# One hybrid attention layer: short attention groups drawn over four ticks, the drain of their sums moved behind the transposed scores, and the split output weights moved from SyncE's queue to ScalarE's

## The reference

```
h = rmsnorm(x); proj = h @ w_in            # q, k, v of 8 stick-breaking heads, q, k, v and gates of 8
                                           # forgetting heads, q of 4 memory heads, a gate over all 20
stick-breaking: A[t,s] = sigmoid(z) * prod_{s<j<t} sigmoid(-z),  s < t, out = A @ v
forgetting:     softmax(q.k + cumulated log forget gates), s <= t,  out = P @ v
memory:         softmax(q.k) over 256 memory rows,                  out = P @ v
y = per-head rmsnorm(outputs) * silu(gate)
out = rmsnorm(x + y @ w_out)
```

## Time and profile before

| | |
|---|---|
| median of 3 runs | 841.03 us |
| the profiled execution | 841.03 us, its span 839.3 us |
| PE busy | 806.2 us (96%) |
| DVE, ACT, POOL busy | 583.5, 474.8, 257.7 us |
| chain that ended last | PE 75%, DVE 11%, ACT 6% |
| mean granted TensorE clock | 0.993 |

### The profile page before, as it was taken

The page is one execution under the profiler, slowest core; times in us unless marked ns, Lnnn a source line. Parts: engine busy times, 40 slices in busy tenths (PEclk is TensorE's granted clock), DMA queues, the critical chain, the costliest instruction groups (busy, mean ns, idle before and its releaser), DMA issues.

```text
span 839.3 us, 12264 instructions
## 1 busy us (share of the span) xinstructions
PE 806.2 (96%) x4244; PEld 676.9 (81%) x4244; DVE 583.5 (70%) x1207; ACT 474.8 (57%) x938; POOL 257.7 (31%) x382
## 2 busy tenths in 40 slices
PE   8899999999999999999999999999999989989996
PEld 7677787887878888887888888788888877878884
DVE  5746667557577877767787776878666584874575
ACT  5756776755855555685555568554555763532231
POOL 1135514232156223415622342562223111420000
PEclk9999999999999999999999999999999998999998
DMA  8125652203313121411312141132213397142532
GB/s 302 52 76 168 203 207 76 72 18 89 114 50 77 53 111 64 120 45 51 76 62 101 64 125 39 52 81 65 93 52 76 125 354 249 34 167 76 176 126 100
DMA packets 35533, 88.95 MB, mean 106 GB/s; under 512 B 3592, under 2 KB 11784, under 8 KB 34448
## 3 DMA queue, kind: packets, MB, share of 16 engines
q1 hardware_dynamic: 35472, 88.17, 31.6%
HBM read 57.72 MB, written 21.53 MB: 94 GB/s over the span
## 4 chain that ended last, share of the span: by engine, by line
PE 75%; DVE 11%; ACT 6%; issue 3%; POOL 3%; DMA 1%; SPq 0%; DVEq 0%; ACTq 0%; POOLq 0%
PE banks L745 13%; PE banks L747 12%; PE banks L746 12%; PE banks L786 9%; PE banks L886 7%; PE banks L906 4%; PE banks L905 4%; PE banks L873 4%; PE banks L872 4%; DVE work L1543 2%; PE banks L926 2%; POOL w_parts L1304 1%; DVE pT L1580 1%; DVE work L1546 1%; DMA work<-in_x 1%
## 5 line engine op out<-in xcount | busy, mean ns | idle before, releaser
L745 PE MATMUL banks<-hT,w_parts 128*128 128x512 f32 x576 | 240.0, 417 | 9.3 <-POOL w_parts L1304 3.2
L747 PE MATMUL banks<-hT,w_parts 128*128 128x512 f32 x576 | 226.1, 392 | 0.0
L746 PE MATMUL banks<-hT,w_parts 128*128 128x512 f32 x576 | 225.3, 391 | 0.0
L1580 DVE TENSOR_TENSOR pT<-banks,pT 128x512 fp32r<-128x512 f32 x208 | 109.1, 563 | 84.2 <-ACT pT L1103 83.1
L1103 ACT ACTIVATE pT<-banks 128x512 fp32r<-128x512 f32 x208 | 93.4, 498 | 130.2 <-PE banks L886 129.6
L745 PEld LDWEIGHTS banks<-hT,w_parts 128*128 128x128 f32 x576 | 108.6, 188 | 26.2 <-DVE fx_heads L1480 4.0
L747 PEld LDWEIGHTS banks<-hT,w_parts 128*128 128x128 f32 x576 | 108.1, 188 | 24.4
L1304 POOL TENSOR_TENSOR w_parts<-w_raw,w_parts 128x1024 fp32r<-128x1024 f32 x37 | 88.8, 2400 | 114.7 <-ACT w_parts L1006 114.7
L746 PEld LDWEIGHTS banks<-hT,w_parts 128*128 128x128 f32 x576 | 109.0, 189 | 12.7
L1079 ACT ACTIVATE work<-banks 128x512 f32<-128x512 f32 (+2 forms) x96 | 47.5, 495 | 96.6 <-PE banks L873 87.6
L1543 DVE TENSOR_TENSOR_SCAN work<-work 128x639 f32<-128x639 f32 (+3 forms) x64 | 92.6, 1446 | 7.2 <-POOL work L1312 7.1
(11 more groups left out here) (213 smaller groups left out, 1395.6 us busy)
## 6 DMA issues: line engine op xcount, KB each, us to landing
w_raw<-in_w_tiles SPq DMA_DIRECT2D x37, 512.0 KB, 3.6
hT<-wo_dram SPq DMA_DIRECT2D x16, 512.0 KB, 7.6
fx_heads<-fx_heads SPq DMA_DIRECT2D x8, 512.0 KB, 7.3
negL<-negL_dram SPq DMA_DIRECT2D x8, 512.0 KB, 7.1
yT_dram<-silu SPq DMA_DIRECT2D x8, 512.0 KB, 5.2
sb_heads<-sb_heads SPq DMA_DIRECT2D x8, 512.0 KB, 7.1
negL<-yT_dram SPq DMA_DIRECT2D x8, 512.0 KB, 5.0
work<-in_x SPq DMA_DIRECT2D x6, 512.0 KB, 6.4
```

Of the source, the lines that this page charges most:

```text
L745: pe.matmul(o, w[:, 0, k, :], hT[:, 0, k, tok], start=(k == 0), stop=False)
L746: pe.matmul(o, w[:, 0, k, :], hT[:, 1, k, tok], start=False, stop=False)
L747: mm = pe.matmul(o, w[:, 1, k, :], hT[:, 0, k, tok], start=False, stop=(k == KT - 1))
L1580: dve.tensor_tensor(pT[:, n % 3, 1, cols], banks[:, T_BANK + n % 2, cols], pT[:, n % 3, 0, cols].bitcast(F32), ALU.subtract).then_inc(t_lo, 1)
```

## The change

Three edits.

1. `t_tick`: the steps of a c=0 group of fx and sb lie one in each of the ticks 4g+5 to 4g+8. The planner, which reads `t_tick`, moves some parts with it.
2. The ten loads and twenty stores of output weight halves, with their waits, go from SP to ACT, in the ticks in which they stood, behind the sigmoids or exponentials (a store behind the rounding, too).
3. `output_lo` on ACT and `output` on DVE stand behind the transposed scores and the small piece of their tick.

```diff
@@ t_tick
-    return 4 * t.group + 5 + (t.s // 2 if x.c else t.s // 2 * 2)
+    return 4 * t.group + 5 + (t.s // 2 if x.c else t.s)
@@ sync: functions load_w_out_half, store_w_out_half and their calls removed
-                for n, half in enumerate(W_OUT_HALF):
-                    if i == half.load:
-                        load_w_out_half(n)
-                    if i == half.store:
-                        store_w_out_half(n)
@@ scalar: the same functions, with act. for sp.
+            def load_w_out_half(i):
+                x, n = W_OUT_HALF[i], halves_before(i)
+                if n:
+                    act.wait_ge(wo_half_out[x.place], 32 * n)
...
+                act.dma_start(wo_half_rows[x.place][0], w_out[...]).then_inc(wo_half_in[x.place], 16)
+            def store_w_out_half(i):
+                x = W_OUT_HALF[i]
+                raw, hi = wo_half_rows[x.place]
+                act.wait_ge(wo_lo, len(W_OUT_AT) + i + 1)
+                act.dma_start(wo_dram[x.j, 0, :, ...], hi).then_inc(wo_half_out[x.place], 16)
+                act.dma_start(wo_dram[x.j, 1, :, ...], raw).then_inc(wo_half_out[x.place], 16)
@@ scalar, tick loop
                 for n, x in enumerate(W_OUT_HALF):
+                    if i == x.load:
+                        load_w_out_half(n)
                     if i == x.split:
                         w_out_half_hi(n)
+                    if i == x.store:
+                        store_w_out_half(n)
...
-                if i in OUT_AT:
-                    output_lo(OUT_AT[i])
                 for n in T_AT[i]:
                     upper_part(n)
                 for n in SMALL_AT[i]:
...
+                if i in OUT_AT:
+                    output_lo(OUT_AT[i])
@@ vector, tick loop
-                if i in OUT_AT:
-                    output(OUT_AT[i])
                 for n in T_AT[i]:
                     lower_part(n)
                 for n in SMALL_AT[i]:
                     finish_small(n)
...
+                if i in OUT_AT:
+                    output(OUT_AT[i])
```

More of the change, by code:

```diff
@@ L583, in store_w_out @@
                 sp.dma_start(wo_dram[j, 1, :, :], wo_rows[j][0]).then_inc(wo_out[j], 16)
[L585 to L604, removed]
             def fetch_w_out(j):
@@ L1170, in w_out_hi @@
                 act.activation(hi.bitcast(F32R), raw, ACT.Copy).then_inc(wo_hi, 1)
+            def load_w_out_half(i):
+                x, n = W_OUT_HALF[i], halves_before(i)
+                if n:
+                    act.wait_ge(wo_half_out[x.place], 32 * n)
+                if x.place == 0:
+                    if x.load // UNITS > 2:
+                        act.wait_ge(sb_p, sb_no(UNITS * (x.load // UNITS)))
+                    act.wait_ge(small_done, small_of("N3", 0, x.load // UNITS - 2) + 1)
+                else:
+                    act.wait_ge(fx_max, fx_no(UNITS * (x.load // UNITS) + UNITS // 2))
+                act.dma_start(wo_half_rows[x.place][0], w_out[wo_rows_of(x.j), x.c * CW:(x.c + 1) * CW]).then_inc(wo_half_in[x.place], 16)
+            def store_w_out_half(i):
+                x = W_OUT_HALF[i]
+                raw, hi = wo_half_rows[x.place]
+                act.wait_ge(wo_lo, len(W_OUT_AT) + i + 1)
+                act.dma_start(wo_dram[x.j, 0, :, x.c * CW:(x.c + 1) * CW], hi).then_inc(wo_half_out[x.place], 16)
+                act.dma_start(wo_dram[x.j, 1, :, x.c * CW:(x.c + 1) * CW], raw).then_inc(wo_half_out[x.place], 16)
             def w_out_half_hi(i):
```

## The result

The changed kernel takes 847.71 us, the median of 4 runs (845.79 to 849.55), beside 841.32 for the kernel before on the same chip: ratio 1.0078, 95% interval 1.0052 to 1.0104. The forecast was 839.8 us with a range up to 844.1. It was wrong, in the sign and by 7.9 us.

The account below looks back on a forecast made before the run. TensorE bounds the kernel, so only its gaps can move the time. The terms -1.5 + 1.35 + 0.5 - 1.0 - 0.2 - 0.4 = -1.25, against 841.03 us, gave 839.8 us, range 836.8 to 844.1.

Parts of the forecast that it names:

- What bounds the kernel: TensorE, busy 806.2 of 839.3 us with unchanged work; time can move only by the gaps in it.
- (a): Gaps at ticks 53, 85, 117, before the first K drain: chain 0.27 shorter, 0.49 us saved each, -1.5 for three.
- (b): Gaps at ticks 59, 91, 123, before the Q drain: one part less as cover, +0.45 us each, +1.35 for three.
- (c): Gaps at ticks 42 and 138, among four `values`: 0.33 of transposes moves behind the gap, +0.23 us each, +0.5 together.
- (d): Gap at tick 141: the last weight tile is split a tick earlier, so the gap goes, -1.0 us.
- (e): Gap at tick 148, where DVE is behind: a one-block `lower_part` leaves, -0.2 us; half clock behind it unchanged.
- (f): Gap at tick 156: fourth part moves out, chain loses a one-block `lower_part`, -0.4 us.
- third rival: The moves cancel, gaps removed in one place open at the next drain: 841.0 us, chance 0.14.
- Edit 2, value 0: Thirty DMA issues on ACT fall into its pauses or hide behind spare time, 1.6 us at tick 77: no change.
- first rival: ACT caught in store issues at ticks 77 and 109, TensorE waits 2.4 and 1.8 us: 844.0 us, chance 0.20.
- Edit 3, value 0, bounds -0.3 to 1.0: Later output where c=1 groups begin: TensorE comes after its old end nearly everywhere, so 0 us, between -0.3 and +1.0.
- second rival: Full clock stays behind the shortened gap of tick 148, 3.0 us more come back: 836.8 us, chance 0.11.

Follow-up runs that it names:

- mixed kernel: Edit 1's steps spread in all phases, parts as before up to tick 127 and edit 1's parts in the last two phases, against before: 838.75 us, ratio 0.9966.

## Why the prediction was wrong, step by step

- **What bounds the kernel**: right. The time moved only by gaps of TensorE and the clock behind them.
- **(a)** Right sign, wrong size: 0.49 each forecast. The gap of tick 85, 0.90 in the earlier trace rows, is 0.79, so 0.11, and the three cost the sum 1.1 us. The term that fails is "the chain is 0.27 shorter". First `scores(83)` and the scan in before, then the same and the `lower_part` that is left with edit 1 alone:

```profile
380.06 0.39 PE L872 MATMUL banks<-sb_heads 128*128 128x512 f32 x1
...
386.92 2.28 DVE L1543 TENSOR_TENSOR_SCAN work<-work 128x1023 f32<-128x1023 f32 x1
```

```profile
380.26 0.39 PE L872 MATMUL banks<-sb_heads 128*128 128x512 f32 x1
...
385.07 0.42 DVE L1580 TENSOR_TENSOR pT<-banks,pT 128x256 fp32r<-128x256 f32 x1 [0.79 <-ACT pT L1103]
...
387.12 2.28 DVE L1543 TENSOR_TENSOR_SCAN work<-work 128x1023 f32<-128x1023 f32 x1
```

  The scan starts 6.86 us behind `scores(83)` in both. DVE has one `lower_part` less ahead of it, but waits 0.79 us for ACT where it waited 0.52: that term is 0. The other two promised 0.34 - 0.12 = 0.22 and gave 0.11.
- **(b)** Right: 0.79 to 1.23, so 0.44 for 0.45, three times.
- **(c)** Right in sign: with edit 1 alone 0.35 us between ticks 32 and 48 and 0.22 between 136 and 140, for 0.23 each. Edit 3 alone adds 0.4 at the same two drains. The formula of `plan` also moves parts at ticks 42, 43 and 130 to 133, which the prediction's list leaves out; at tick 42 as many parts stand in front of `values` as before.
- **(d)** Right: the gap is gone, -1.01 for -1.0.
- **(e), (f)** The gap of tick 148 went from 3.04 to 2.71 us, so -0.33 for -0.2, and that of tick 156 from 2.29 to 1.95, so -0.34 for -0.4. The half clock behind tick 148, "taken as unchanged", was 3.5 us in place of 6.9; edit 3 adds 0.4 at tick 146. Together they make the -0.84 of the table.
- **Edit 1 as a whole.** The measured terms sum to about -0.1 us where the forecast had -1.25, and edit 1 alone shows just that: a ratio of 1.0000. Nearly all of the miss is (a). So the **third rival**, "the moves cancel", was right for edit 1.
- **Edit 2, value 0**: right for the edit alone (841.86), wrong beside edit 1. The step that failed is "ACT ends it at 351.4 and DVE takes it at 352.93, so 1.6 us are free". These were rows of before, at tick 77, where ACT rounds steps 2 and 3 of the short group a tick earlier. Edit 1 moves the rounding of step 3 into the very tick ahead of the stores, and ACT stops there for TensorE. At tick 109 this took 1.3 us of ACT's lead (from 1.25 us ahead of `scores(109)` to 0.06 behind it), before any store. I priced each edit against before and added.
- **The first rival** (844.0, 0.20) had the mechanism, the place and nearly the price of the chain: its ticks 77 and 109 with 2.4 and 1.8 us. It came at tick 109 alone, with 2.35 us, and with 1.7 of half clock behind that I had not counted there. At tick 77 SP's K copy took the long issue (2.85 us) and ACT's stores 0.33 and 0.55. What I held against it, that ACT's own queue would be empty, protects the first store of a pair only: the second took 3.02.
- **Edit 3, value 0, bounds -0.3 to 1.0**: a step that failed as much. 3.1 us alone. "TensorE comes 0.7 us or more after the old end nearly everywhere" was read at the starts of long groups of fx and sb; the memory phases, where a group's output falls every four ticks of 2.2 us, were not looked at (about 2.0 us). Nor does it fit ticks 42 and 138, where `values` already waited, as (c) says itself. And "the three operations take as long in either order" is true and beside the point: `values` waits for the first `lower_part` only, so the order decides whether two or three stand in front of it (0.4 us at three ticks).
- **The second rival** (clock stays up behind tick 148): partly right. In the profile of edit 1 alone (838.36 us, mean clock 0.997) the clock stays up behind a gap of 2.68 us, and in the mixed kernel behind 2.67; with the same gap it falls in others. A single execution can go either way, but the shares differ: the eight other kernels with edit 1, whole or in part, have 50 of 76 runs at 0.995 or above, before has 27 of 83. Which of the gaps that edit 1 shortens does this was not tested.
- **The range** failed with the missed costs: with edit 3 at 3.1 and edit 2 beside the other two at 4.8, -1.25 becomes 6.7, measured 6.4. That it comes so near is in part luck: edit 1 was forecast 1.1 us too low, and edits 1 and 3 cost about 1 us less together than apart.

## What to carry to other kernels

Price an edit against the kernel that the other edits leave, above all where one edit delays an engine and another puts work on its queue: edits 1 and 2 were worth nothing alone and cost 2.2 us as a pair, and beside edit 3 as well edit 2 costs 4.8. When an operation is moved behind another, ask what the waiting engine needs first, not when all of them end, and look at the phase with the shortest ticks. Put DMA issues where nothing urgent stands behind them on the same engine: the kernel with the same six stores took 847.7 us with them in front of a drain, 843.6 with them at the end of the tick and 843.1 with them on SP.

## What the runs showed of the hardware

**The length of an issue.** One 256 KB store took from 0.33 to 3.24 us to issue. What was in flight matters: at tick 45 with edit 2 alone the pair came 3.6 us ahead of the K copies (two of 512 KB) and took 0.33 and 0.45 us. Its place in the queue matters too. On ACT the first store of a pair took 0.33 or 0.34 us in all fifteen pairs of ticks 45, 77 and 109 (five profiles), and only the second was long. On SP, where the pair stands directly behind another 512 KB copy, the first took 2.0 us or more each time. The second store on ACT at tick 109, by its distance behind the second K copy's issue, took 0.98 us at 1.8 (edits 2 and 3), 1.76 at 2.5, 3.02 at 3.1, 2.29 at 3.8 and 0.50 at 6.5 us; at the other two ticks the lengths do not follow that distance so (1.64 at 3.8, tick 77 with edits 1 and 2). The `yT_dram` copy, 512 KB as well, is issued between, and which of the copies counts was not tested. No other queue was issuing in the 3.02 us: SP's last issue had ended at 501.67, ACT's began at 501.89. The Trainium skill ("Perfetto Trace Analysis", section "DMA Instruction — HWDGE (DVE, Sync)") says that an issue's duration holds the wait for the descriptor generator's lock and the generation itself, and draws the descriptor buffer as full with the engines starting early. By the row a lock held by another queue can't be the reason here; a full buffer would fit, and no run isolates it. The Trainium skill ("DMA: Bandwidth & Descriptors", section "Issuing engines are not separate DMA queues") says that a second issuing engine saves only sequencer time, usually small beside the DMA. Here the sequencer's time was not small beside the DMA: 3.02 of the 7.1 us from the store's issue to its landing, against 0.45 of 2.3 us at tick 45 with edit 2 alone. That a store on ACT's queue lands so much later behind SP's copies fits shared engines; no run isolates it.

**The clock behind a gap.** Gaps of 1.9 to 3.1 us are followed by 3.4, 3.5 or 6.9 us at 1.2 GHz in some executions and not in others: by 6.9 us at 0.51 behind tick 148's gap of 3.04 us in before, but not behind the gap of 2.67 us in the mixed kernel, whose window right behind it is

```profile
690.30:697.00 6.70, 6.70 (x36) 5.74 (x37) 3.10 (x6) 2.22 (x5) 0.54 (x2) 1.00 1.02 390
```

while its next gap, of 1.87 us at 704.6, was followed by half clock (0.69 in the mean of the 5.5 us from 704.5). What decides it stays open.
